# A mixture-of-experts decoder step: spreading expert rows back to tokens with one f32 product in place of three bf16 ones, an announced branch and a reordered last round

## The reference

```python
scores = sigmoid(x @ w_router)
idx    = top 8 of scores + bias, within the best 4 of 8 groups
wsel   = scores[idx] / sum(scores[idx]) * 2.5
routed = sum over the chosen e of wsel[e] * ((silu(x @ w_gate[e]) * (x @ w_up[e])) @ w_down[e])
x      = x + g2 * (routed + swiglu(x, ws_gate, ws_up, ws_down))
```

## Time and profile before

| | us |
|---|---|
| median of three runs | 1608.26 |
| the profiled execution | 1608.05 |
| its span, first to last instruction | 1605.8 |
| busy: TensorE / its weight loads | 1516.5 / 1005.8 |
| busy: VectorE / ScalarE / GpSimd | 712.7 / 363.6 / 94.2 |

### The profile page before, as it was taken

How to read it: one execution, slowest core, us unless ns; L and a number is a source line. 1 busy time by engine, 2 the same in 40 slices (tenths; PEclk the granted TensorE clock), 3 DMA queues, 4 the chain that set the end, 5 groups by cost and what they waited for, 6 DMA issues and landing times. The chain is left out here.

```text
span 1605.8 us, 29569 instructions
## 1 busy us (share of the span) xinstructions
PE 1516.5 (94%) x11206; PEld 1005.8 (63%) x11206; DVE 712.7 (44%) x2012; ACT 363.6 (23%) x770; POOL 94.2 (6%) x119
## 2 busy tenths in 40 slices
PE   6999998999999999999997899999999999999986
PEld 4778765686665665566554587766665556556543
DVE  3205535215465445445355335443745434543463
ACT  3012443203112112112111345332112111111111
POOL 0000110001000000000000000001000000010000
PEclk9999999999999999999999999999999999999998
DMA  9997699329999999999989983988999999999895
GB/s 364 388 370 269 254 397 402 136 81 403 361 418 421 419 421 421 420 419 419 408 354 411 359 260 124 367 318 337 418 419 420 420 420 420 420 418 408 335 419 216
DMA packets 153584, 580.30 MB, mean 361 GB/s; under 512 B 17181, under 2 KB 62401, under 8 KB 105226
## 3 DMA queue, kind: packets, MB, share of 16 engines
q1 hardware_dynamic: 137642, 535.74, 84.3%
q0 software_dynamic: 15200, 40.92, 6.6%
q10 hardware_dynamic: 640, 2.26, 0.4%
HBM read 567.17 MB, written 26.90 MB: 370 GB/s over the span
## 5 line engine op out<-in xcount | busy, mean ns | idle before, releaser
L2471 PE MATMUL ps<-ring,scratch 128*64 128x256 f32 x3296 | 367.5, 380 | 9.0 <-DMA ring<-in_moe_w_up 7.8
L2471 PEld LDWEIGHTS ps<-ring,scratch 128*64 128x64 f32 x3296 | 244.3, 137 | 118.7 <-issue 12.9
L2537 PE MATMUL ps<-ring,scratch 128*64 128x512 f32 x896 | 200.5, 598 | 0.3 <-DVE scratch L2851 0.3
L693 PE MATMUL ps<-hT,ring 128*128 128x264 f32 x768 | 180.5, 389 | 1.3 <-ACT hT L379 1.3
L2434 PE MATMUL ps<-scratch 128*128 128x264 bf16 x1392 | 170.6, 276 | 2.1 <-DVE xT L2761 2.0
L2786 DVE SCALAR_TENSOR_TENSOR scratch<-scratch,ps 128x256 f32<-128x256 f32 x62 | 29.8, 481 | 318.7 <-ACT scratch L2888 312.2
L693 PEld LDWEIGHTS ps<-hT,ring 128*128 128x128 f32 x768 | 146.0, 192 | 30.7 <-issue 2.5
L2434 PEld LDWEIGHTS ps<-scratch 128*128 128x128 bf16 x1392 | 121.8, 97 | 52.1 <-issue 15.0
L2537 PEld LDWEIGHTS ps<-ring,scratch 128*64 128x64 f32 x896 | 58.2, 136 | 118.0 <-issue 87.7
L2753 DVE TENSOR_TENSOR scratch<-scratch,ps 128x264 f32<-128x264 f32 x224 | 96.4, 430 | 66.4 <-PE ps L2434 64.4
L2888 ACT ACTIVATE scratch<-ps 128x256 f32<-128x256 f32 x62 | 23.9, 385 | 426.5 <-PE ps L2471 355.1
(11 more groups left out here) (402 smaller groups left out, 1486.1 us busy)
## 6 DMA issues: line engine op xcount, KB each, us to landing
ring<-in_moe_w_up SPq DMA_DIRECT2D x128, 1024.0 KB, 21.3
ring<-in_moe_w_gate SPq DMA_DIRECT2D x126, 1024.0 KB, 19.8
ring<-in_moe_w_down SPq DMA_DIRECT2D x120, 1024.0 KB
ring<-in_ada_w SPq DMA_DIRECT2D x48, 1024.0 KB, 12.8
ring<-in_ret_w_in SPq DMA_DIRECT2D x24, 1024.0 KB, 17.1
ring<-in_state_ret SPq DMA_DIRECT2D x16, 1024.0 KB, 14.2
out_ret_sample<-ring POOLq DMA_DIRECT2D x16, 1024.0 KB, 9.0
ring<-in_gla_w_in SPq DMA_DIRECT2D x12, 1024.0 KB, 13.1
```

What stands on the lines that cost most here:

```text
L693: mm = nc.tensor.matmul(k.ps[:, bank, 0:T], w[:, c, m * P:(m + 1) * P], k.h[:, c, :], start=(c == 0), stop=(c == DC - 1))
L2471: mm = nc.tensor.matmul(k.ps[lo:lo + CAP, 2 + p, j * DE:(j + 1) * DE], xg[:, p, c, lo:lo + CAP], w[:, c, :], start=(c == 0), stop=(c == DC ...
L2537: mm = nc.tensor.matmul(k.ps[lo:lo + CAP, 6 + half, :], hid_t[:, p, m, lo:lo + CAP], slot(k, n, D)[:, m, half * 512:(half + 1) * 512], sta ...
```

## The change

In all rounds the rows stay f32 (`rows_of`) and the one-hot matrix is f32 too (`slot_token`, `token_of`). ScalarE's copy is all that is left of the making of parts; VectorE's three passes (L2851, L2854, L2841) go, and `s_rhi`, `s_rest` and `s_mid` with them: their waiters wait for `s_part`, which ScalarE's copy now counts. The spread has one f32 product for each tile and chunk. In the heavy round `next_slots` moves ahead of where the passes were. In the last round both down halves come before the whole last spread, with the follow-ups from chunk 2 on. The `If` and `Else` of each engine become a compare-and-branch with blocks written out, and its place is announced to the engine (`mark_branch_hint_location`) at the start of round 14 (GpSimd: of round 15). Buffers are laid out anew; the loop over extra tiles is changed in the same way as the spread. Loads, their order, and the numbers of all other products stay.

```diff
@@ spread
             for p in range(n):
-                for s in range(3):
-                    mm = nc.tensor.matmul(k.ps[:, c % 2, 0:T], parts_of(p)[:, s, c * P:(c + 1) * P],
-                                          slot_token[:, p, :], start=(p == 0 and s == 0),
-                                          stop=(p == n - 1 and s == 2))
+                mm = nc.tensor.matmul(k.ps[:, c % 2, 0:T], rows_of[:, p, c * P:(c + 1) * P], token_of(p),
+                                      start=(p == 0), stop=(p == n - 1))
             mm.then_inc(s_scat, 1)
@@ scalar_round
-            if last:
-                nc.scalar.copy(last_rows[:, cols], k.ps[:, 6 + half, :]).then_inc(s_part, 1)
-                continue
-            nc.scalar.copy(parts_of(p)[:, 0, cols], k.ps[:, 6 + half, :]).then_inc(s_rhi, 1)
+            nc.scalar.copy(rows_of[:, p, cols], k.ps[:, 6 + half, :]).then_inc(s_part, 1)
@@ vector_round
-        for q in range(0 if last else 2 * tiles(r)):
...
-            nc.vector.tensor_tensor(rest[:, half], k.ps[:, 6 + half, :], parts_of(p)[:, 0, cols],
-                                    ALU.subtract).then_inc(s_rest, 1)
...
-            nc.vector.tensor_copy(parts_of(p)[:, 1, cols], rest[:, half]).then_inc(s_mid, 1)
-            low_part(q)
-            if heavy and q == 1:
-                next_slots(v, r + 2, of)
+        if heavy:
+            next_slots(v, r + 2, of)
@@ pe_round, down products
                 if p:
-                    pe.wait_ge(s_rest, 2 * d + 2 * (p - 1) + half + 1)
+                    pe.wait_ge(s_part, 2 * d + 2 * (p - 1) + half + 1)
@@ last_spread
+        wait_light(pe, LAST, "moe_w_down")
+        four_down(0, LIGHT_BLOCKS, 1, LIGHT_PLACE)
         for half in range(2):
-            if half:
-                wait_light(pe, LAST, "moe_w_down")
-                four_down(0, LIGHT_BLOCKS, 1, LIGHT_PLACE)
-                if follow:
-                    follow(pe, 0)
-                    follow(pe, 1)
             pe.wait_ge(s_part, 2 * d + 1 + half)
             for c in range(4 * half, 4 * half + 4):
                 pe.wait_ge(s_add, DC * (LAST + 1) + c - 1)
...
-                if half and follow:
+                if c >= 2 and follow:
                     follow(pe, c - 2)
@@ the branch
+    def announce_branch(eng, name):
+        hints[name] = eng.mark_branch_hint_location()
+    def branch(eng, name, pairs, twice=False):
+        here = bass.OrderedEngineSet([eng.engine])
+        more, done = f"{tag}_{name}_extra", f"{tag}_{name}_joined"
+        usual = f"{tag}_{name}_usual" if twice else done
+        eng.br_cmp(pairs, 0, on_true=usual, on_false=more, comp_op="IS_LE").branch_hint(hints[name])
+        return (here, more, usual, done) if twice else (here, more, done)
```

More of the change, by code:

```diff
@@ L2553, in pe_round @@
             for half in range(2):
-                pe.wait_ge(s_rest, 2 * d + 2 * (PAIRS - 1) + half + 1)
+                pe.wait_ge(s_part, 2 * d + 2 * (PAIRS - 1) + half + 1)
                 four_down(PAIRS, HEAVY_BLOCKS, half)
@@ L2639, in rounds_tensor @@
         for r in range(HEAVY - 2, LAST):
+            if r == LAST - 1:
+                announce_branch(pe, "pe")
             pe_round(pe, r)
@@ L3016, in rounds_vector @@
         for r in range(HEAVY - 2, LAST):
+            if r == LAST - 1:
+                announce_branch(v, "v")
             vector_round(v, r)
@@ L3087, in tail_sync @@
         pairs = extra_pairs["sp"]
-        with sp.If(pairs > 0):
+        here, more, done = branch(sp, "sp", pairs)
+        with nc.body(more, valid_engines=here):
             for i in range(KEPT):
@@ L3098, in tail_sync @@
             sp.wait_ge(s_final if layer else nxt.s_sum, 2 if layer else 1)
+            sp.br(done)
+        nc.switch_bb(done)
         load_until(k, sp, n_end + RING)
@@ L3105, in tail_pool @@
         pairs = extra_pairs["pool"]
-        with pool.If(pairs > 0):
+        here, more, done = branch(pool, "pool", pairs)
+        with nc.body(more, valid_engines=here):
             with pool.Fori(0, pairs) as i:
@@ L3110, in tail_pool @@
                 fetch_rows(pool, 0, x_row)
+            pool.br(done)
+        nc.switch_bb(done)
     def tail_tensor(pe):
@@ L3131, in tail_tensor @@
         pairs = extra_pairs["pe"]
-        with pe.If(pairs > 0):
+        here, more, usual, done = branch(pe, "pe", pairs, twice=True)
+        with nc.body(more, valid_engines=here):
             pe_round(pe, LAST)
@@ L3176, in tail_tensor @@
                         pe.wait_ge(x_add, DC * i + DC + c - 1)
-                    for s in range(3):
-                        mm = nc.tensor.matmul(k.ps[:, 2 + c % 2, 0:T], row_parts[:, 0, s, c * P:(c + 1) * P],
-                                              slot_token[:, 0, :], start=(s == 0), stop=(s == 2))
-                    mm.then_inc(x_scat, 1)
+                    nc.tensor.matmul(k.ps[:, 2 + c % 2, 0:T], rows_of[:, 0, c * P:(c + 1) * P],
+                                     slot_token[:, 0, :], start=True, stop=True).then_inc(x_scat, 1)
             pe.wait_ge(x_add, pairs * DC + DC)
@@ L3183, in tail_tensor @@
                 follow(pe, c)
-        with pe.Else():
+            pe.br(done)
+        with nc.body(usual, valid_engines=here):
             pe_round(pe, LAST)
@@ L3206, in tail_vector @@
         linked = k.dve.n
-        with v.If(pairs > 0):
+        here, more, usual, done = branch(v, "v", pairs, twice=True)
+        with nc.body(more, valid_engines=here):
             finish()
@@ L3243, in tail_vector @@
                         .then_inc(x_add, 1)
+            v.br(done)
         k.dve.n = linked
-        with v.Else():
+        with nc.body(usual, valid_engines=here):
             finish()
+            v.br(done)
+        nc.switch_bb(done)
         if layer == 0:
@@ L3254, in tail_scalar @@
         pairs = extra_pairs["act"]
-        with act.If(pairs > 0):
+        here, more, usual, done = branch(act, "act", pairs, twice=True)
+        with nc.body(more, valid_engines=here):
             scalar_round(act, LAST)
@@ L3273, in tail_scalar @@
                     act.wait_ge(x_dn, 2 * i + half + 1)
-                    nc.scalar.copy(row_parts[:, 0, 0, half * 512:(half + 1) * 512], k.ps[:, 6 + half, :])\
-                        .then_inc(x_hi, 1)
+                    nc.scalar.copy(rows_of[:, 0, half * 512:(half + 1) * 512], k.ps[:, 6 + half, :])\
+                        .then_inc(x_part, 1)
             if layer == 0:
@@ L3279, in tail_scalar @@
                     nxt.square(act, c)
-        with act.Else():
+            act.br(done)
+        with nc.body(usual, valid_engines=here):
             scalar_round(act, LAST)
```

68 lines of the change are left out of this document (23 added, 45 removed).

## The result

The changed kernel takes 1636.14 us (median of 4 runs, 1634.91 to 1638.77), the kernel before beside it 1607.66 (4 runs): a ratio of 1.0177, with an interval of 1.0163 to 1.0191. It is slower by 28.5 us, and 1636.14 lies above the forecast range of 1620 to 1632. The profiled execution took 1634.91 us. These are lines of its page: span, busy time, rate of the transfers in 40 slices, and the chain that ended last by engine.

A forecast was written before the change was run, and what follows sets the result against it. The weights bound ordinary rounds (31.2 us against TensorE's 30.33); dearer f32 products were to make TensorE the bound at 31.8. Layer 0's +11.5 and layer 1's +6.6 sum to 18.1 us on 1608.05, so 1626; range 1620 to 1632.

The forecast's parts named there:

- The price of the product: Spread on TensorE: one f32 product takes 0.445 us against 0.35 for three bf16 ones; a two-tile spread grows 1.45 us.
- The rival of dearer products: Spread: 0.47 us a product, 1.85 us more a round, 4.8 us more a layer with the heavy rounds, 1636; chance 8%.
- Rounds 1 to 11: Ordinary expert rounds: TensorE's 31.8 us exceeds the weights' 31.2; the last ordinary round's spread comes 9.5 and 8.5 us later.
- the hinge: Ordinary rounds: TensorE needs 30.33 us, the weights 31.2; adding more than 0.87 us to TensorE's round turns the bound.
- What the removed work gives: VectorE's three passes dropped per tile and half: counted 0 to -0.3 us a round, taken as 0.
- Heavy round to last gates: Two more two-tile spreads add 2.9 us; the weight stream restarts 12.4 and 11.4 us late; gates wait under 1 us.
- The last ups: Last round's up products, behind the one-tile spread: weights land at 890.0 and 1585.2, spread ends at 889.3 and 1584.5.
- The landing of the last down weights: End of each expert stage: down weights land 19.4 us after the gates, moving to 899.7 and 1594.9.
- The tail: Last round's end: second down halves end at 901.6 and 1596.8; layer 0 ends +11.5 us, layer 1 +6.6.
- What follows the halves: Last spread's 8 chunks with follow-ups behind both down halves: 8.2 and 6.9 us, against 7.2 and 5.1 before.
- The branch: Last gates: with the branch announced they take 3.66 us in both layers; saved 2.2 and 7.0 us become up-weight wait.
- the fetch stays: Behind the branch: TensorE starts last gates 5.7 us after ready, 1629.5; 1635 with a stop within the gates; chance 12%.

The follow-up runs named there:

- fifth: The kernel before with four bf16 products in place of three, the smallest part spread twice, not in the last spread: 1649.13 us, ratio 1.025.
- sixth: The kernel before with two bf16 products a tile and chunk, the smallest part made but not spread: 1601.04 us, ratio 0.996.
- seventh experiment: The changed kernel with VectorE's three passes put back on scratch data nobody reads: 1637.64 us, ratio 1.019 to the kernel before.
- third experiment: The kernel before with both down halves ahead of the last spread, bf16 parts and branch as before: 1606.75 us, ratio 0.9996.
- first experiment: The changed kernel with the old order of the last spread (four chunks, second down half, four chunks): 1630.94 us, ratio 1.0141 to the kernel before.
- fourth experiment: The kernel before with f32 rows and products alone, old branch and old order: 1640.18 us, ratio 1.02.
- the second: The kernel before with the announced branch alone, on every engine: 1602.17 us, ratio 0.9954.
- ninth experiment: The kernel before with the announced branch and two bf16 products, the smallest part left out of the ordinary spreads: 1602.18 us, ratio 0.9957.

## Why the prediction was wrong in its size

The direction and the main mechanism were right: the change is slower since two records a product make the spread dearer, TensorE takes the pace from the weights, and the work saved on VectorE is worth nothing. The forecast of +18.1 us for the two stages measured 29.5 in the profiles, 6.2 too little in layer 0 and 5.2 in layer 1. Step by step:

- **The price of the product** was mis-sized. It was taken as 0.445 us and the two-tile spread as +1.45 us. From one spread's start to the next instruction is 448.94 - 441.69 = 7.25 us, and before it was 449.40 - 443.76 = 5.64: +1.61. The block with the row of 0.445 (L2573) has no change of bank or tile between its products, the spread has; that this is the reason no run shows. A round of 31.97 us in place of 31.8 is 1.7 us over ten rounds, and with the heavy round's spreads 1.9 us in each layer. The rival of dearer products gave 1636, the measured time, but with 1.85 us a round; that was not what happened, so its hit is luck, and 1.61 explains only 3.8 of the missing 11.4 us.
- **Rounds 1 to 11**: right in kind. No wait for ups, the rate at 399 to 419 GB/s. The fifth and sixth experiments show the hinge at 31 us from both sides.
- **What the removed work gives**: 0 was right, by the seventh experiment for VectorE's load, and by the 0.3 us of the kernel before for the wait that went with it.
- **Heavy round to last gates**: right. The release came 14.3 and 13.3 us later against U1, where 12.4 and 11.4 were forecast, which is the 1.9 above. The wait for the last gates is none and 0.20 us. The last ups were forecast to wait 0.7 us and didn't: the one-tile spread ahead of them took 5.6 us, not 5.3.
- **The landing of the last down weights** was put too early. I had taken 19.4 us after the gates from the drop of the rate to 99 GB/s, since the kernel before doesn't wait for them. Where a kernel does wait, the second half starts, counted from SyncE's issue at the release, in layer 0 after 77.1 us (third experiment, 887.41 - 810.27), 77.3 (changed) and 77.2 (first experiment, 902.98 - 825.83), and in layer 1 after 76.4 (changed, 1613.43 - 1537.04). The forecast amounts to 75.4 and 75.2. So the stream is no slower than before; I read its end 1.9 and 1.2 us too early.
- **The tail**, "the second halves end at 901.6 and 1596.8", was the step that failed in kind. It let each second half take 1.9 us behind the wait. With the terms above the wait is 3.82 and 2.64 us instead of 2.5 and 2.5, and the clock falls in it: 3.64 and 3.65 us, 1.7 more in each layer. A hint of it stood in the prediction: the last gates took 5.88 us at a clock of 0.50 after 4.75 us without work. I had used it for the gates and not asked the same of the wait that the new order makes, though for one as short as 2.5 us no row stood there. What follows the halves takes 8.9 us in layer 0 and 7.2 in layer 1 (to 1624.31, where TensorE is ready for L1942), 0.7 and 0.3 more than the 8.2 and 6.9 I had written; the terms written there add up to 7.6 and 6.7 only.
- **The branch**: right for TensorE in layer 0, where the last gates take 3.57 us. In layer 1 a stop of 1.01 us stayed within them, so 5.18 and not 3.66; the second halves behind it started when their weights landed, so it cost nothing here. The Trainium skill (Runtime: NRT & Kernel Launch, "Instruction fetch mechanics") says that prefetch is sequential; with the place announced, TensorE's stops of 3.79 and 4.35 us ahead of the last gates (fourth experiment) are gone in the first, so by that rule alone the trace doesn't go. The one within the gates of layer 1 stays: 1.30 us there, 1.16 in the first, 1.01 in the changed kernel. The rival "the fetch stays" is refuted for the engine that counts, but for this last.

For layer 0 the terms are 1.9 (product) + 1.9 (landing) + 1.7 (clock) + 0.7 (follow-ups) = 6.2, of 6.2 missing; for layer 1 1.9 + 1.2 + 1.7 + 0.3 = 5.1, of 5.2. The last 1.2 us between 27.3 in the spans and 28.5 in the medians is that of single executions.

What I missed beside the sum is how the three edits hang together. The f32 product alone costs 31.6 us, more than the whole change, since it removes the wait that hid the stop at the branch. The announced branch gives back 9.2 of it, and the order takes 6.1 again.

Open: what in the announced branch removes TensorE's stop; and why layer 0 needs 0.8 us longer than layer 1 from the release to the landing. The loads queued behind the last down halves differ, several against one, but no run changed them.

## What to carry to other kernels

Count a product's passes before trading several bf16 products for one f32: here an f32 product took the time of four, so three parts are the cheaper way as long as making them is hidden, as it was. Going below three parts shortens a round only where TensorE sets the pace. A stop that lies under a wait is free until the wait goes, so when an edit delays an engine against its stream, price every stop behind it anew. Keep small independent work between two waits for late transfers: it costs nothing while the engine waits, and it can save both the wait and the half-speed block behind it.

## What the runs showed of the hardware

- **The clock after a wait.** Waits of TensorE of 2.64, 3.35, 3.63, 3.82, 3.85, 4.36 and 4.51 us were followed by a block that ran at half clock for all or part of it: 1.9 us of work became 3.5 to 3.65, 3.6 became 5.35 to 6.5. After 1.87 us (third experiment) the clock stayed at full speed, but so it did after 3.36 us in layer 1 of the second (1568.61, 3.68 us for the block), where the same 3.36 us in layer 0 of the sixth were followed by 5.34. In the changed kernel a wait of 1.97 us, for VectorE at the head of round 14's transposes, stands in both layers; the down products behind it take 5.34 us in layer 0 and 3.64 in layer 1. So the wait's length alone doesn't decide it, and no run here says what does.
- **The scatter of one kernel goes with the clock.** Of the 17 executions of the kernel before beside the ninth experiment the fastest took 1605.32 us at a mean granted clock of 0.995, the slowest 1614.42 at 0.986. A difference of a few us between two single executions proves nothing.
- **VectorE's stop behind the branch follows something other than the announcement.** In layer 0 of the changed kernel VectorE stops for issue before its first instruction behind the branch, with TensorE's stop gone. These are VectorE's rows there and in layer 1, then that of layer 1 in the kernel before, then that of layer 0 in the fourth experiment, both not announced:

```profile
881.85 0.20 DVE L2195 SCALAR_TENSOR_TENSOR scratch<-ps,tab 128x36 f32<-128x36 f32 x1 [5.61 <-issue]
...
1594.63 0.20 DVE L2195 SCALAR_TENSOR_TENSOR scratch<-ps,tab 128x36 f32<-128x36 f32 x1 [5.50 <-issue]
```

```profile
1562.77 0.20 DVE L2186 SCALAR_TENSOR_TENSOR scratch<-ps,tab 128x36 f32<-128x36 f32 x1 [0.52 <-issue]
```

```profile
881.33 0.20 DVE L2181 SCALAR_TENSOR_TENSOR scratch<-ps,tab 128x36 f32<-128x36 f32 x1 [0.56 <-issue]
```

In layer 0 of the kernel before it was 5.74 us. VectorE's place is announced at the start of round 14, as TensorE's is. The stop is long (5.4 to 5.8 us) with and without announcement, and short (0.5 to 0.6 us) with and without it: in layer 1 it is short in all kernels with bf16 parts and in the seventh experiment. What decides it no run shows. Where VectorE is on the way, as in the seventh experiment, it is 4.92 us of TensorE's time.
